# Product-key experts: the first tile's query projections split into 32 tokens and 96 tokens

## The reference, cut to what matters

```
def peer_ffn(h, w_q, sub_keys, u, v):        # T = 512 tokens, 8 heads, top 16
    q = (ht @ w_q).reshape(T, 8, 2, 128)      # w_q: 1024 x 2048
    s = einsum('thpc,hpnc->thpn', q, sub_keys)           # 128 keys for each of two halves
    v1, i1 = top_k(s[:, :, 0], 16); v2, i2 = top_k(s[:, :, 1], 16)
    cand, cand_idx = all 16 x 16 sums of v1, v2, and i1 * 128 + i2
    top_s, pos = top_k(cand, 16); idx = cand_idx at pos; g = softmax(top_s)
    a = einsum('thkd,td->thk', u[idx], ht)                # gather 128 rows of u a token
    return einsum('thk,thkd->td', gelu(a) * g, v[idx])    # and of v
```

## Time and profile before

| | |
|---|---|
| timed runs | 3292.05, 3299.95, 3301.63 us (median 3299.95) |
| profiled execution, its own time | 3293.69 us |
| its span | 3291.9 us |
| TensorE busy | 2581.9 us, 78% of the span |
| VectorE busy | 2048.9 us, 62% |
| ScalarE busy | 736.8 us, 22% |
| GpSimd busy | 649.0 us, 20% |
| DMA, mean over the span | 246 GB/s |

### The profile page before, as it was taken

The page is one execution under the profiler, slowest core; times in us unless marked ns, Lnnn a source line. Parts: engine busy times, 40 slices in busy tenths (PEclk is TensorE's granted clock), DMA queues, the critical chain, the costliest instruction groups (busy, mean ns, idle before and its releaser), DMA issues. The chain is left out here.

```text
span 3291.9 us, 34612 instructions
## 1 busy us (share of the span) xinstructions
PE 2581.9 (78%) x13120; PEld 1490.9 (45%) x13120; DVE 2048.9 (62%) x4464; ACT 736.8 (22%) x1676; POOL 649.0 (20%) x649
## 2 busy tenths in 40 slices
PE   9999899895333453434575779999999998999998
PEld 4554545441000121101132347458844476878887
DVE  6676831777777777677776439547487686465422
ACT  2144211222111222212343221122111232211000
POOL 1211000344444444444444310000000000000000
PEclk9999999997656666657787889999999999999999
DMA  6764212799999999999999983022255563122222
GB/s 213 259 238 159 77 64 90 305 420 409 421 421 419 416 417 417 419 416 419 416 418 415 420 340 124 26 80 77 90 192 214 204 224 124 64 88 80 89 90 77
DMA packets 120567, 810.93 MB, mean 246 GB/s; under 512 B 13936, under 2 KB 16496, under 8 KB 32464
## 3 DMA queue, kind: packets, MB, share of 16 engines
q0 software_dynamic: 91312, 619.09, 46.6%
q1 hardware_dynamic: 29088, 189.62, 15.5%
HBM read 779.30 MB, written 29.36 MB: 246 GB/s over the span
## 5 line engine op out<-in xcount | busy, mean ns | idle before, releaser
L1471 PE MATMUL po<-pair,diag 128*32 128x512 f32 x1868 | 432.6, 925 | 495.4 <-ACT diag L1588 495.0
L1742 DVE SCALAR_TENSOR_TENSOR pair<-pair,shared 128x1024 f32<-128x1024 f32 x467 | 566.7, 1225 | 327.4 <-DMA pair<-in_peer_uv,idx 315.1
L1296 POOL DMA_INDIRECT pair<-in_peer_uv,idx x467 | 529.1, 1133 | 859.7 <-PE po L1471 540.8
L1471 PEld LDWEIGHTS po<-pair,diag 128*32 128x32 f32 x1868 | 77.5, 145 | 731.7 <-ACT diag L1588 581.2
L1583 ACT ACTIVATE ge<-a 128x4 f32<-128x4 f32 (+1 forms) x130 | 26.7, 205 | 949.3 <-DVE pair L1742 929.4
L1471 PE MATMUL po<-shared,diag 128*32 128x512 f32 x180 | 144.9, 953 | 109.3 <-ACT diag L1588 109.3
L2175 PE MATMUL acc<-a,ring 128*128 128x512 f32 x512 | 220.9, 592 | 0.0
L2175 PEld LDWEIGHTS acc<-a,ring 128*128 128x128 f32 x512 | 97.3, 190 | 122.0 <-issue 122.0
L1862 DVE TENSOR_TENSOR weight_sums<-ring 128x512 f32<-128x512 f32 x53 | 36.7, 692 | 167.5 <-DMA ring<-in_w_fc 151.3
L1886 PE MATMUL bank<-hT,ring 128*128 128x256 f32 x592 | 139.9, 379 | 0.0
L1886 PE MATMUL bank<-hT,weight_sums 128*128 128x256 f32 x592 | 139.8, 379 | 0.0
(11 more groups left out here) (543 smaller groups left out, 4547.7 us busy)
## 6 DMA issues: line engine op xcount, KB each, us to landing
ring<-in_w_fc SPq DMA_DIRECT2D x62, 1024.0 KB, 4.8
mg<-in_ada_w POOLq DMA_DIRECT2D x96, 512.0 KB, 5.0
tab<-s_tables SPq DMA_DIRECT2D x16, 1664.0 KB, 6.4
first<-in_w_first SPq DMA_DIRECT2D x14, 1024.0 KB, 7.1
other<-in_w_first SPq DMA_DIRECT2D x14, 1024.0 KB, 6.9
s_tables<-weight_sums POOLq DMA_DIRECT2D x8, 1664.0 KB, 6.6
s_tables<-table POOLq DMA_DIRECT2D x8, 1664.0 KB, 6.2
shared<-in_w SPq DMA_DIRECT2D x10, 1024.0 KB, 16.1
```

The source lines that it names most:

```text
L1296: pool.indirect_dma_start(out=place[at], out_offset=None, in_=core.dram["peer_uv"][:, :], in_offset=bass.IndirectOffsetOnAxis(ap=idx[:, su ...
L1471: last = pe.matmul(po[j * TOK:(j + 1) * TOK, t % 2, half * 512:(half + 1) * 512], diag[:, g % 3, i, :], place[at][:, D + half * 512:D + (h ...
L1742: dve.scalar_tensor_tensor(row, row, 1.0, h_rows[:, t % 2, j, :], ALU.mult, ALU.mult, accum_out=a[:, g % 4, i:i + 1]).then_inc(dotted, 1)
```

## The change

`project_first` gets a token range. TensorE makes all eight pieces for the first 32 tokens (unit 0's, TOK = 32), then score(0), then all eight again for the other 96 tokens, then score(1), all eight tokens(n), and score(2). ScalarE copies each bank twice, once for each range, with exponentials(0) between the copies of the second range. `first_made` and `first_taken` now count to 4; score(1) to score(3) wait for 4.

```
-            def project_first(i):
+            def project_first(i, lo, hi):
-                if i == 0:
+                if lo == 0 and i == 0:
                     pe.wait_ge(core.first_landed, 16 * fetched)
-                elif i % 2 == 0:
+                elif lo == 0 and i % 2 == 0:
                     pe.wait_ge(core.peer_landed[i // 2], 16)
                 for k in range(KT):
-                    if i == 0:
+                    if lo == 0 and i == 0:
                         pe.wait_ge(normed, k + 1)
-                    last = pe.matmul(acc[:, i // 4, i % 4 * P:(i % 4 + 1) * P], ring[i // 2][...],
-                                     core.hT[:, k, 0:P], ...)
+                    last = pe.matmul(acc[:, i // 4, i % 4 * P + lo:i % 4 * P + hi], ring[i // 2][...],
+                                     core.hT[:, k, lo:hi], ...)
...
             def project_rest(i):
                 if i < 2:
-                    pe.wait_ge(first_taken, i + 1)
+                    pe.wait_ge(first_taken, i + 3)
...
             def score(u):
                 if u < QUAD:
-                    pe.wait_ge(first_taken, 2)
+                    pe.wait_ge(first_taken, 4 if u else 2)
...
             for i in range(8):
-                project_first(i)
+                project_first(i, 0, TOK)
             pe.wait_ge(core.peer_landed[0], 16)
             score(0)
-            tokens(0)
-            tokens(1)
-            tokens(2)
-            tokens(3)
+            for i in range(8):
+                project_first(i, TOK, P)
             score(1)
-            for n in range(4, 2 * QUAD):
+            for n in range(2 * QUAD):
                 tokens(n)
             score(2)
...
-            def take_first(b):
-                act.wait_ge(first_made, b + 1)
-                act.activation(qT[:, 4 * b:4 * b + 4, 0:P], acc[:, b, :]..., ACT.Copy).then_inc(first_taken, 1)
+            def take_first(part_, b):
+                lo, hi = ((0, TOK), (TOK, P))[part_]
+                act.wait_ge(first_made, 2 * part_ + b + 1)
+                act.activation(qT[:, 4 * b:4 * b + 4, lo:hi], acc[:, b, :]...[:, :, lo:hi], ACT.Copy).then_inc(first_taken, 1)
...
-            take_first(0)
-            take_first(1)
+            take_first(0, 0)
+            take_first(0, 1)
             score(0)
-            for n in range(4):
-                tokens(n)
+            take_first(1, 0)
+            exponentials(0)
+            take_first(1, 1)
             score(1)
-            exponentials(0)
-            for n in range(4, 2 * QUAD):
+            for n in range(2 * QUAD):
                 tokens(n)
             score(2)
             exponentials(1)
```

More of the change, by code:

```diff
@@ L1302, in _ @@
         def _(pe):
-            def project_first(i):
-                if i == 0:
+            def project_first(i, lo, hi):
+                if lo == 0 and i == 0:
                     pe.wait_ge(core.first_landed, 16 * fetched)
-                elif i % 2 == 0:
+                elif lo == 0 and i % 2 == 0:
                     pe.wait_ge(core.peer_landed[i // 2], 16)
                 for k in range(KT):
-                    if i == 0:
+                    if lo == 0 and i == 0:
                         pe.wait_ge(normed, k + 1)
-                    last = pe.matmul(acc[:, i // 4, i % 4 * P:(i % 4 + 1) * P], ring[i // 2][:, k * 256 + i % 2 * P:k * 256 + (i % 2 + 1) * P],
-                                     core.hT[:, k, 0:P], start=(k == 0), stop=(k == KT - 1), skip_group_check=True)
+                    last = pe.matmul(acc[:, i // 4, i % 4 * P + lo:i % 4 * P + hi], ring[i // 2][:, k * 256 + i % 2 * P:k * 256 + (i % 2 + 1) * P],
+                                     core.hT[:, k, lo:hi], start=(k == 0), stop=(k == KT - 1), skip_group_check=True)
                 if i % 4 == 3:
@@ L1503, in _ @@
         def _(act):
-            def take_first(b):
-                act.wait_ge(first_made, b + 1)
-                act.activation(qT[:, 4 * b:4 * b + 4, 0:P], acc[:, b, :].rearrange("p (i s) -> p i s", i=4), ACT.Copy).then_inc(first_taken, 1)
+            def take_first(part_, b):
+                lo, hi = ((0, TOK), (TOK, P))[part_]
+                act.wait_ge(first_made, 2 * part_ + b + 1)
+                act.activation(qT[:, 4 * b:4 * b + 4, lo:hi], acc[:, b, :].rearrange("p (i s) -> p i s", i=4)[:, :, lo:hi],
+                               ACT.Copy).then_inc(first_taken, 1)
             def take_rest(i):
```

## The result

The change makes the kernel slower: median 3329.19 us of six runs (3319.63 to 3331.91) against 3300.79 of six before (3292.05 to 3306.36), ratio 1.0084 with a 95% interval of 1.0069 to 1.0100, or 28 us. The forecast was 3328: 31 us on a time before of 3297.

The account below looks back on a forecast made before the run. Gathers of expert rows bound the stage, and the tenth, waiting for TensorE's first group, moves the end. Terms 9.6 - 0.3 + 0.4 + 17.3 + 0.7 + 3 = +31 us on 3297 gave 3328 us, range 3307 to 3352.

Parts of the forecast that it names:

- first pass: L1312 with 32 columns on TensorE: clock stays low to the end, 27 us against 17.45 before, +9.6.
- copy, score 0: ScalarE's smaller first copies save 0.3 us; score 0 on TensorE at the low clock costs 0.4 more.
- second pass: L1312 with 96 columns, wholly new: 6.6 us at the low clock, then 96 x 0.112 at full, +17.3.
- wait before score 1: TensorE now waits for the second pass's copy and two handovers before score 1: +0.7 us.
- tiles with scores 1 and 2: Token tiles behind the second pass: about three in gather traffic at 5 us, five at 1.8, +3 us.
- L1325 and the first group: Later projections and the first group's work on TensorE up to the tenth gather: unchanged, 0.
- The bound: Expert stage bound by gathers; what moves the tenth gather moves the stage's end by the same amount, +31 us.
- Rival D: Expert stage: the delay is hidden because later gathers make up for it; about 3298 us, chance 0.04.
- The narrow matmul: L1312: weight load sets the pace, 0.112 us at 32 or 96 columns; 32 columns hardly raise the clock.
- Rival A: L1312: the clock rises in the first pass as before; +19 us, 3316 us, chance 0.18.
- Rival C: L1312: a narrow matmul costs by its moving columns; between -6 and +7 us, about 3297, chance 0.06.
- Rival B: L1312: the clock stays low in the second pass too, 27 us for 17.3; sum +45, 3342 us, chance 0.30.

Follow-up runs that it names:

- the two reorderings: Kernel before with the change's order on TensorE but no split, exponentials(0) on ScalarE ahead of all token tiles or behind tile 3: ratios 1.0023 and 0.9989.
- wide_twice: The changed kernel with both passes at all 128 columns, so every piece is made twice: ratio 1.0038 to the kernel before.
- split_96_32: The changed kernel split at token 96 in place of 32, so 96 columns first and 32 second: ratio 1.0072 to the kernel before.
- fill_more: fill_waits with project_rest(2) moved behind the first group's sums and score(3) ahead of them: ratio 0.9987 to the kernel before.
- hold_gathers: The kernel before with GpSimd's first gather waiting until all eight token tiles are copied: ratio 0.9996 to the kernel before.
- fill_waits: Kernel before with project_rest(0) between token tiles 5 and 6, project_rest(1) between 6 and 7, exponentials(1) ahead of tile 6, score(3) behind project_rest(2): ratio 0.9982.

## Why the prediction was right

Its terms against the two profiles, in us on the way to the tenth gather:

| step | predicted | measured | from |
|---|---|---|---|
| first pass | +9.6 | +9.9 | matmul records, 27.37 less 17.45 |
| copy, score 0 | +0.1 | +0.3 | copies of 0.28; pass end to next matmul 1.47 against 1.21 |
| second pass | +17.3 | +17.1 | 587.85 to 604.95 |
| wait before score 1 | +0.7 | +1.9 | 604.95 to 606.85 |
| tiles with scores 1 and 2 | +3 | -2.4 | 19.5 against 22.0 |
| L1325 and the first group | 0 | -1.0 | to the tenth gather, 24.3 against 25.3 |
| sum | +31 | +25.7 | D |

*The bound.* Right for this change. The tenth gather carries the end: in the change, the two reorderings, wide_twice and split_96_32 the shift of the last gather against the kernel before equals that of the tenth within 0.5 us. Rival D is out: over the 1296 us from the tenth gather to the last nothing was made up. It is no rule for every order, though: in fill_more 9.9 us at the tenth gather were 3.5 at the last.

*The narrow matmul.* Right, both halves. The load sets the pace (0.112 us with 32 columns at full clock, split_96_32). At the low level the pace is 0.213 and not the 0.205 of the prediction, which was a mean over 32 instructions not all at that level; taking 27 and not 26.2 made this good. By the Trainium skill, "TensorE: Matmul & The Clock Gate", LDWEIGHTS, 128 weight columns take about 128 / 1.2 = 107 ns. The trace's spacing of 112 is near that at full clock, but at the low level it has 213, twice that. The clock stayed low through all of the narrow pass, and wide_twice shows that this, not the count of instructions, is what the first pass pays for. Rival A fell with that. For it had stood what the same page of the Trainium skill says in "What's actually happening", that the clock is set by how busy the engine has been recently. If busy is what the profile counts as busy, this trace does not agree: TensorE was busy for 20.38 of 20.40 us and was not given its full clock. Rival C needed under 0.1 us an instruction; the two passes took 44.5 us for 256, 0.174 each, and it is out.

*The second pass.* The middle choice, a rise after some 6 us at 96 columns, was met (6.39 us for the first 32). Rival B's case, a low clock throughout, did not come in the change or in split_96_32.

*The token tiles.* Here a term was wrong, and not in size alone: "about three tiles in traffic and five at 1.8" gave +3, and it measured -2.4. ScalarE's timeline after shows one late tile:

```profile
616.85 0.60 ACT L1525 ACTIVATE shared<-pt 128x512 f32<-128x512 f32 x1 [1.20 <-PE pt L1363]
620.36 0.60 ACT L1525 ACTIVATE shared<-pt 128x512 f32<-128x512 f32 x1 [2.91 <-remote]
```

Its step is 3.51 us, two more take 2.65 at the low clock, and the other four are the normal 1.80. The first three tiles were copied on time while the first six gathers were still landing, at a DMA share of 1.01 (see hold_gathers). So one of the prediction's own signs of being wrong came true, tiles on time under gathers: it took the late signals to go with traffic, and by where they lie they go with GpSimd's issues. 5 us a tile was too much as well. The sum was 5 us over D, in the main for this; the -1.0 in the row of L1325 is its first call, which before ran longer at the low clock (6.92 us, 5.92 after).

The wait before score 1 is longer than predicted for the same kind of reason. The second pass ends at 604.95, but the signal for its last copy, right behind the issue of the sixth gather, comes 1.35 us later; in the first pass, with no gather begun, it came at once (586.38, copy at 586.41):

```profile
606.30 0.49 ACT L1505 ACTIVATE qT<-acc 128x384 f32<-128x384 f32 x1 [7.78 <-PE acc L1312]
```

The time itself moved by 28 us with an interval of 23 to 33, which holds both the sum of 31 and D's 25.7. That 3328 was hit to 1 us is luck: the time before that it started from, 3297, was 4 us under the median of six runs, and the 31 us added were 3 too many.

*What the change did.* Unit 0's experts were named at 597.06 after 583.53 before: even the part that was meant to come early came 13.5 us later, or 10 without the later start (the prediction had about 9).

## What to carry to other kernels

Splitting these float32 matmuls along their moving columns saved nothing, since the weight load set the pace (0.112 us for 32 as for 128 columns), and it paid every load again: before such a split, compare a row with fewer columns and the same weights. Here the stretch of 32-column matmuls cost twice, since the clock failed to rise in it (the change) or fell in it (split_96_32), and it was 11 us slower than the same matmuls made wide with the surplus thrown away (wide_twice). Where transfers bind a stage, look for the wait that opens the stream, and check that the next waits move with it (fill_waits against fill_more); here the gain was in filling TensorE's handovers, 6 us by the timed runs.

## What the runs showed of the hardware that I had not expected

- In split_96_32 the clock that fell in the narrow pass stayed at 0.50 for 44 us, through all eight token tiles (1.94 us each in place of 1.08), until the long projections. The narrow stretch so made what followed it slow too.
- The end signals of token tiles came late beside GpSimd's issues of gathers (up to 4.8 us, before at 592.77) and not beside the gathers' traffic alone (0.05 to 0.07 us at a DMA share of 1.01). Before, three tiles in a row were late, by 1.1, 4.8 and 2.1 us; in the change it was one of eight, by 1.8, and one copy of projections, by 1.35. Not every signal in such a stretch is late.
- Behind the last gather the nine profiled executions take either about 1375 or about 1383 us. Timed runs of one kernel differ by 9 to 16 us; whether this is the reason I did not test.
